# Head pairs of three attentions: the values become the stationary operand, in two column halves of TensorE

## The reference, cut to what matters

```python
# odd layer, selected and window branch (16 heads, groups of 4 share keys and values)
s = einsum(q, k) * scale - slopes * (t - position)
p = masked_softmax(s, causal)
o = einsum(p, v);  o_layer = g0 * o_cmp + g1 * o_slc + g2 * o_win
# second block: memory attention (256 keys) and selected attention (top-k of the causal keys)
p = softmax(einsum(qm, km) * MEM_DH ** -0.5);  out = einsum(p, vm)
p = softmax(where(valid, einsum(qb, kg) * SA_DH ** -0.5, -inf));  out = einsum(p, vg)
```

## Time and profile before

| | |
|---|---|
| median of 3 runs | 1486.98 us (1486.61 to 1489.99) |
| the profiled execution | 1486.23 us, of which its span is 1484.4 us |
| TensorE (PE) busy | 1429.5 us, 96% of the span |
| VectorE, ScalarE, GpSimd busy | 592.7, 600.2, 626.2 us |
| mean granted TensorE clock | 0.991 of full speed |

### The profile page before, as it was taken

The page is one execution under the profiler, slowest core; times in us unless marked ns, Lnnn a source line. Parts: engine busy times, 40 slices in busy tenths (PEclk is TensorE's granted clock), DMA queues, the critical chain, the costliest instruction groups (busy, mean ns, idle before and its releaser), DMA issues.

```text
span 1484.4 us, 20224 instructions
## 1 busy us (share of the span) xinstructions
PE 1429.5 (96%) x7598; PEld 1163.8 (78%) x7601; DVE 592.7 (40%) x1130; ACT 600.2 (40%) x1131; POOL 626.2 (42%) x345
## 2 busy tenths in 40 slices
PE   6999999999999999999999998988999999999999
PEld 4787886878778787888887677877788888888887
DVE  1114104632452255666434678779422322323000
ACT  5112232634123337666434574545334433433210
POOL 3763543654346523233344672621144434444441
PEclk9999999999999999999999999999999999999999
DMA  7543522022234410003033232103023232332330
GB/s 197 118 94 100 124 89 66 1 51 72 85 114 137 119 57 15 21 25 94 29 87 115 85 87 78 57 15 114 15 86 92 93 99 86 95 100 87 99 113 29
DMA packets 78402, 120.28 MB, mean 81 GB/s; under 512 B 8449, under 2 KB 41393, under 8 KB 77937
## 3 DMA queue, kind: packets, MB, share of 16 engines
q1 hardware_dynamic: 76096, 114.21, 26.6%
q0 software_dynamic: 2208, 4.98, 1.2%
q10 hardware_dynamic: 16, 0.00, 0.0%
HBM read 114.95 MB, written 4.19 MB: 80 GB/s over the span
## 4 chain that ended last, share of the span: by engine, by line
PE 79%; issue 7%; POOL 5%; DVE 3%; ACT 2%; DVEq 1%; DMA 1%; POOLq 1%; ACTq 0%; SPq 0%
PE psum L1636 20%; PE psum L1638 19%; PE psum L1637 19%; PE psum L1682 5%; PE psum L1668 3%; POOL weight_low L455 3%; PE psum L1648 3%; PE psum L1615 2%; PE psum L1784 1%; PE psum L1983 1%; PE psum L1959 1%; PE psum L1771 1%; POOL rstd L479 1%; DVEq L1363 1%; DMA x_tokens<-in_x 1%
## 5 line engine op out<-in xcount | busy, mean ns | idle before, releaser
L455 POOL TENSOR_TENSOR weight_low<-weight_raw,weight_high 128x1024 fp32r<-128x1024 f32 x188 | 459.2, 2446 | 613.7 <-ACT weight_high L675 313.8
L1636 PE MATMUL psum<-act_ring,weight_high 128*128 128x512 f32 x704 | 282.4, 401 | 0.4 <-issue 0.4
L1638 PE MATMUL psum<-act_ring,weight_low 128*128 128x512 f32 x704 | 277.3, 394 | 0.0
L1637 PE MATMUL psum<-act_ring,weight_high 128*128 128x512 f32 x704 | 277.0, 394 | 0.0
L675 ACT ACTIVATE weight_high<-weight_raw 128x1024 fp32r<-128x1024 f32 x104 | 109.9, 1060 | 387.3 <-PE psum L1638 378.9
L1636 PE MATMUL psum<-weight_high,act_ring 128*128 128x512 f32 x480 | 193.4, 403 | 2.9 <-DVE odd_k L1243 2.3
L1638 PE MATMUL psum<-weight_high,act_ring 128*128 128x512 f32 x480 | 190.2, 396 | 0.0
L1637 PE MATMUL psum<-weight_low,act_ring 128*128 128x512 f32 x480 | 190.2, 396 | 0.0
L1636 PEld LDWEIGHTS psum<-act_ring,weight_high 128*128 128x128 f32 x704 | 132.4, 188 | 35.7 <-issue 5.1
L1638 PEld LDWEIGHTS psum<-act_ring,weight_low 128*128 128x128 f32 x704 | 132.3, 188 | 34.1
L1637 PEld LDWEIGHTS psum<-act_ring,weight_high 128*128 128x128 f32 x704 | 132.4, 188 | 30.4
(11 more groups left out here) (332 smaller groups left out, 2145.6 us busy)
## 6 DMA issues: line engine op xcount, KB each, us to landing
weight_raw<-in_w_ffn_in SPq DMA_DIRECT2D x88, 256.0 KB
weight_raw<-in_even_w_in SPq DMA_DIRECT2D x32, 512.0 KB
weight_raw<-in_w_in SPq DMA_DIRECT2D x24, 512.0 KB
weight_raw<-in_w_ffn_out SPq DMA_DIRECT2D x22, 512.0 KB
weight_raw<-in_odd_w_in SPq DMA_DIRECT2D x20, 512.0 KB
weight_raw<-in_even_w_out SPq DMA_DIRECT2D x8, 512.0 KB
weight_raw<-in_odd_w_in SPq DMA_DIRECT2D x16, 256.0 KB
weight_raw<-in_odd_w_out SPq DMA_DIRECT2D x8, 512.0 KB
```

The source lines that it names most:

```text
L455: nc.gpsimd.tensor_tensor(WL[:, r], RAW[:, r], WH[:, r].bitcast(f32), ALU.subtract).then_inc(split_ready, 1)
L1636: mm(bank, hi_l, hi_r, start=start, stop=False, skip_group_check=True)
L1637: mm(bank, hi_l, lo_r, start=False, stop=False, skip_group_check=True)
L1638: return mm(bank, lo_l, hi_r, start=False, stop=stop, skip_group_check=True)
```

## The change

In the odd, memory and selected attention (not in the first layer) the two operands of the value products change places. The steps s and s+1 of two neighbouring query tiles make a **half** n of 256 queries. For each block of 128 keys the values (128 x 64) are stationary and the turned probabilities of up to 256 queries stream: h = 0 in columns 0 to 63 of the array, h = 1 in columns 64 to 127. The result is turned: head dimension on partitions (h = 0 on 0 to 63, h = 1 on 64 to 127), 512 queries of a pair along a bank. ScalarE copies that bank to SBUF (`pair_copy`), TensorE turns it back in four transposes (`pair_back`), and VectorE takes the pair as before. In the diff, `pair_copy` is ScalarE's, the lines on `pair_back` with `dve` are VectorE's, and `half_values`, `pair_back` and the loop are TensorE's.

```diff
+        def probs_t(s, h):
+            if s // 2 % 2 == 0:
+                half = A_PT[:, h].rearrange("p a (b q) -> p (a b) q", b=2)
+            elif s < SEC_FIRST:
+                half = O_PT[h]
+            else:
+                half = G_F[:, 4 + 2 * h:6 + 2 * h, :].rearrange("p a (b q) -> p (a b) q", b=2)
+            at = P * (step_tile(s) % 2)
+            return half, half[:, 0:step_width(s) // P, at:at + P]
...
+        def half_free(eng, s):
+            n = (s - FOX_UNITS) // 2
+            if n >= 2:
+                eng.wait_ge(sem("half_values"), n - 1)
+            elif n >= 0:
+                eng.wait_ge(sem("pair_values"), FOX_UNITS)
...
+            def pair_copy(s, first):
+                p, last = divmod(s - 6, 4)
+                if first and s >= first + 6 and last == 0:
+                    act.wait_ge(sem("half_values"), 2 * (p - FOX_UNITS // 4) + 2)
+                    nc.scalar.activation(pair_t(p), PS[:, 6 + p % 2, :], ACT.Copy).then_inc(sem("pair_out"), 1)
...
                 if s >= s0 + 7 and last == 0:
-                    dve.wait_ge(sem("pair_values"), 4 * p + 4)
+                    if s0:
+                        dve.wait_ge(sem("pair_back"), p - FOX_UNITS // 4 + 1)
+                    else:
+                        dve.wait_ge(sem("pair_values"), 4 * p + 4)
...
+            def half_values(n, value):
+                s0 = FOX_UNITS + 2 * n
+                p, late = s0 // 4, n % 2
+                if not late:
+                    pe.wait_ge(sem("pair_done"), p - 1)
+                keys = 2 if SEC_FIRST <= s0 < SEC_FIRST + MEM_UNITS else 2 * late + 2
+                for h in range(2):
+                    pe.wait_ge(sem("pair_pt_b" if h else "pair_pt"), s0 + 2)
+                for t in range(keys):
+                    first = P if t and t == keys - 1 and keys == 2 * late + 2 and s0 not in range(
+                        SEC_FIRST, SEC_FIRST + MEM_UNITS) else 0
+                    for h in range(2):
+                        last = mm(PS[rows_of(h), 6 + p % 2, 2 * P * late + first:2 * P * late + 2 * P], value(h, t),
+                                  probs_t(s0, h)[0][:, t, first:2 * P], start=t == 0, stop=t == keys - 1,
+                                  skip_group_check=True)
+                last.then_inc(sem("half_values"), 1)
+
+            def pair_back(p):
+                pe.wait_ge(sem("pair_out"), p - FOX_UNITS // 4 + 1)
+                for t in range(NT):
+                    last = nc.tensor.transpose(PS[:, 6 + p % 2, P * t:P * t + P], pair_t(p)[:, P * t:P * t + P],
+                                               ID[:, :])
+                last.then_inc(sem("pair_back"), 1)
...
-            for u in range(ODD_UNITS + 3):
+            for u in range(ODD_UNITS + 4):
...
-                if u >= 3:
+                if u >= 4 and u % 2 == 0:
                     i, gp = (u - 3) // 16, (u - 3) // 4 % 4
                     col = 256 * SNAKE[i % 2][gp][0] + HD * i
-                    pair_values(s - 3, lambda h, t, col=col: O_V[:, t, col:col + HD])
+                    half_values(u // 2 - 2, lambda h, t, col=col: O_V[:, t, col:col + HD])
+                if u >= 7 and u % 4 == 3:
+                    pair_back((s - 7) // 4)
```

More of the change, by code:

```diff
@@ L230, in program @@
         lay_b.close()
+        O_PT, O_OT = [None, None], [None, None]
+        lay_b = ExitStack()
+        O_PT[0] = sb(lay_b, "odd_probs_t_a", [P, NT, 2 * P])
+        O_OT[0] = sb(lay_b, "odd_pair_t0", [P, T])
+        lay_b.close()
         W2 = sb(lay_o, "cmp_w2", [P, 2, 2, HD])
@@ L263, in program @@
         G_L = sb(lay_l, "hg_log_forget", [P, 4, T])
+        lay_l.close()
+        lay_l = ExitStack()
+        S_OT = sb(lay_l, "sec_pair_t", [P, 2, T])
         lay_l.close()
@@ L742, in pair_exp @@
                                              sem("pair_probs"), 1)
+                pair_copy(s, first)
             def high(block, i, r):
@@ L918, in _ @@
             act.wait_ge(sem("cmp_taken"), 2 * NT)
-            for s in range(ODD_UNITS + 2):
+            for s in range(ODD_UNITS + 3):
                 pair_exp(FOX_UNITS + s, FOX_UNITS, SEC_FIRST)
@@ L974, in _ @@
                 split_and_take("hg_n", i, G_N[:, :, 512 * i:512 * i + 512], beside_hg, (ACT.Identity, ACT.Silu)[i], "sec")
-            for s in range(SEC_FIRST, SEC_FIRST + MEM_UNITS + SA_UNITS + 2):
+            for s in range(SEC_FIRST, SEC_FIRST + MEM_UNITS + SA_UNITS + 3):
                 pair_exp(s, SEC_FIRST, SEC_FIRST + MEM_UNITS + SA_UNITS)
@@ L1099, in pair_step @@
                     dve.wait_ge(sem("pair_turned"), 2 * k + 1)
-                    if k >= 2:
-                        dve.wait_ge(sem("pair_values"), k - 1)
-                    v.tensor_copy(A_PT[:, k % 2, 0, 0:n], PS[:, 4, 0:n]).then_inc(sem("pair_pt"), 1)
+                    if k >= FOX_UNITS:
+                        half_free(dve, k)
+                        v.tensor_copy(probs_t(k, 0)[1], PS[:, 4, 0:n].rearrange("p (t q) -> p t q", q=P)).then_inc(
+                            sem("pair_pt"), 1)
+                    else:
+                        if k >= 2:
+                            dve.wait_ge(sem("pair_values"), k - 1)
+                        v.tensor_copy(A_PT[:, k % 2, 0, 0:n], PS[:, 4, 0:n]).then_inc(sem("pair_pt"), 1)
                 if s < s0 + steps:
@@ L2085, in _ @@
             pe.wait_ge(sem("sa_features"), 8)
-            for s in range(SEC_FIRST, SEC_FIRST + MEM_UNITS + SA_UNITS + 3):
+            for s in range(SEC_FIRST, SEC_FIRST + MEM_UNITS + SA_UNITS + 4):
                 if s < SEC_FIRST + MEM_UNITS + SA_UNITS:
```

33 lines of the change are left out of this document (24 added, 9 removed).

## The result

The kernel with the change takes a median of 1469.33 us (4 runs, 1468.20 to 1472.47), the kernel before 1488.39 us on the same chip (4 runs, 1486.61 to 1489.99). The ratio is 0.9865, with a 95% interval of 0.9852 to 0.9879: faster by 1.2 to 1.5%. The profiled execution took 1469.13 us; that of before had taken 1486.23, so between the two traces 17.1 us are to be found. (The four runs of before are 1486.6, 1487.0, 1489.8 and 1490.0; two of them lie over 3 us above its profiled one, and so the medians stand 19 apart.)

What follows compares the result with a forecast made beforehand. PE, busy 96% of the span, was taken to bound the kernel; -17 us in the odd layer and -1 in the second block, from 1486.2, gave 1468.5 for the profile and 1469 for the median, range 1462 to 1488.

Steps and rivals of the forecast that it cites:

- What bounds: Whole kernel: PE is busy 96% of the span; the odd layer is PE's alone, the memory attention partly VectorE's.
- Do the column halves run side by side?: New value products: both heads' streams run abreast, as row halves do; early half 0.85 us, late half 1.71.
- Turning back: After each pair's values on PE: four transposes plus the return to the scores' row halves, 0.53 us.
- One change of shape more, 0.1: PE's pair: the step without values goes straight from turning to scores, adding 0.1 us; PE's pair sums to 8.26 us.
- PE waits 0.18 in each pair: Odd layer's 512-key scores: the loop through VectorE and ScalarE takes 5.34 us, PE's work 5.16; the pair takes 8.44.
- waits of PE that rise from 4 to 8 us: Sign of a right forecast in the odd stretch's timeline: PE's waits rise to 8 us or so, most at scores behind exponentials.
- covered by a tenth of a us: ScalarE's new copy: the turning back needs it 0.9 us after the late half, and PE has 1.0 of other work.
- Rival 3: ScalarE's copy tour binds: each pair loses about 0.5 us more, 1477; chance 0.75 together with the forecast.
- Ends and high parts: Odd layer: uncovered stage end +1.7 us, nine steps with high parts +1, first steps without values +0.5; layer -17.
- Second block: Memory attention gains nothing; selected attention gains 2 x 1.4 us, given back by an end of 1.7; sum -1.
- Rival 1: Value products: 64-wide loads stand in the open, +1.3 us a pair; about 1485, no change that can be told; chance 0.09.
- Rival 2: Value products: the column halves run one after another, +0.72 us a pair; 1486.2 + 16 = 1502; chance 0.16.

Runs made afterwards that it cites:

- experiment 1: The change, but both heads write their values to partitions 0 to 63, so both use one column half of the array: 1506.63 us, ratio 1.0119 to the kernel before.
- experiment 8: The change, but TensorE turns every pair back twice, eight transposes in place of four: 1475.99 us, ratio 0.9897 to the kernel before.
- experiment 7: The change without ScalarE's copy and the four transposes back; VectorE takes the turned bank as it is: 1469.42 us, ratio 0.9853 to the kernel before.
- experiment 10: The change without copy and turning back, with VectorE taking a finished odd-layer pair one step later: 1463.28 us, ratio 0.9814 to the kernel before.
- experiment 6: The change, but ScalarE copies each pair's bank twice: 1482.01 us, ratio 0.9946 to the kernel before.
- experiment 5: The change in the odd layer alone; memory and selected attention keep the old way: 1471.69 us, ratio 0.9882 to the kernel before.
- experiment 4: The change, but each query tile streams by itself, 128 columns at a time, 20 passes a pair in place of 12: 1470.18 us, ratio 0.9878 to the kernel before.
- experiment 9: The change, but VectorE takes a finished odd-layer pair one step later, behind the second 256-key maximum: 1469.34 us, ratio 0.9851 to the kernel before.
- experiment 2: The change, but in each half all key blocks of head 0 come first, then all of head 1: 1486.87 us, ratio 0.9986 to the kernel before.

## Why the prediction was right, point by point

The forecast was 1469 for the median and 1468.5 for the profile; they are 1469.33 and 1469.13. (Its own sum, 1486.2 less 18, gives 1468.2.) Faster by over 0.3% had 0.79. The mechanism was right; that the numbers agree within a us is partly luck. The forecast was -18, and the traces are 17.1 apart, the medians 19.1; the median of before has itself risen by 1.4 since the forecast used it, and several terms were off and cancelled. The steps, one by one:

- **What bounds.** That the odd layer is PE's alone held: PE's shorter pair came out whole in the time, 9.70 to 8.44 us.
- **Do the column halves run side by side?** Taken from the row halves, as the nearest row in kind. Right, and better than there: starts 0.01 apart, the streams back to back. The late half was put at 1.71 (1.66), the early one at 0.85 (0.80). The terms of the streams, 1.51 and 0.65, were exact (experiment 1); the 0.2 for the first load and the change of shape is 0.15.
- **Turning back**: 0.53 forecast, 0.58 measured.
- **"One change of shape more, 0.1"** was the mis-sized term. The turning ahead of a half now takes 1.02 for eight transposes and 0.59 for four, where it took 0.93 and 0.49: the first record of a 64-column product starts some 0.1 us later behind a transpose than that of a 128-column one did. No wait for a copy is in this: in experiment 8, where the other engines have more time, they are 1.03 and 0.58. The change has two such places in each pair besides the one counted. TensorE's pair is 8.41 us (experiment 8), not 8.26.
- **"PE waits 0.18 in each pair"** was mis-sized the other way: the wait is 0.03 (8.44 less 8.41). Its sign, waits of PE that rise from 4 to 8 us, most of them at scores behind an exponential, did not come: the rows make 5.5 us where before's make 4.5, and what is new stands in the last pair. The loop itself was priced well: from the 384-key scores to the 512-key scores 5.34 forecast, 5.30 in the timeline (636.04 to 641.34), and experiments 7 and 10 show that it needs 8.43 and that VectorE's taking of the pair, named in the forecast's chain, is in it. The sum 8.44 is right because the pair is the longer of the two, and the loop's was right; the too small value for TensorE stood under it. That is luck: a forecast by TensorE's pair alone would have been 0.15 x 16 = 2.4 us too low. Whether the 0.03 is a wait for the loop or for ScalarE's copy is not told apart.
- **ScalarE's copy "covered by a tenth of a us"**: by 0.02 at most (experiment 6). The forecast let the copy start 0.2 after the late half; it starts 0.38 after, because the second 512-key exponential is in front. Rival 3 was nearer than said.
- **Ends and high parts**: forecast +3.2 against 16 x -1.26. -17 was forecast for the stage, -17.9 measured. The end costs 1.0 us with the last pair's own saving already taken off, where -1.26 + 1.7 = 0.4 was forecast. The first period saved 1.7 (10.66 to 8.99), where 1.26 - 0.5 = 0.8 was forecast; by what the other kernels show of this period, it says little. The steps with high parts cost 0.13 in three pairs and 0.33 in one, of which one pair before had 0.31 as well: +0.4 for the +1 forecast. Experiment 8 shows that they are waits for another engine.
- **Second block**: -1 forecast, -1.0 measured, by other parts. Memory attention was to give nothing and costs 0.5 (the offset goes from -16.05 at its first scores to -15.53 at the selected attention's first), the last 512-key scores stand at -18.16 (-2.6 for the -2.8 forecast), and the end costs 1.1 for 1.7. In the memory attention PE, behind waits of 0.9, 0.3, 0.2 and 1.2 us, ran at a mean clock of 0.66 from 1007 to 1012 us. The values of a half take 1.02 us at the full clock (1003.17 to 1004.19) and 1.91 there (1008.93 to 1010.84):

```profile
1003.17 1.08 PE L1758 MATMUL psum<-pair_probs_t,mem_k_v 128*64 128x256 f32 x8
...
1008.93 1.98 PE L1758 MATMUL psum<-hg_q_f,mem_k_v 128*64 128x256 f32 x8
```

Such a stretch shows in the traces of eleven of the twelve kernels whose second block was changed (not in experiment 1's), and neither in the kernel before nor in experiment 5, which leave that block as it was. So it looks like a cost of the change that no term of the forecast has; no run takes it away alone.
- **What was not foreseen** besides: the stretch at 1.2 GHz between the stages, +1.5 us in this profile. It stands against the 0.9 that the odd stage won beyond its forecast.
- **Rival 1, loads in the open.** Records within a head follow at the pitch of the stream, and experiment 4 adds 16 loads a pair for nothing. The Trainium skill (TensorE: Matmul & The Clock Gate, The mechanism) says that a weight load overlaps a running matmul only where the row groups differ; here all loads share all row groups with two running products, and none shows. The measurement decides against the rule in this form.
- **Rival 2, one after another**: not so, but its price was near (16 us over the kernel before given, 17.8 measured when forced).

## What to carry to other kernels

Where the output of a float32 product has only 64 columns on the stationary side, two independent ones in the two column halves cost the time of one (here with 128 rows, and streams of 128 and 256 columns); put the small operand there, let the long one stream, and alternate between the halves every one to four records; eight in a row cost 0.9 us a half here, and nothing between was tried. Price a change of this kind by the streamed columns at their pitch plus 0.1 us for each new switch between 128- and 64-column products, and the turning back where the layout must be kept.

After TensorE's share is cut, find the length of the next loop before the next cut: adding work to one engine (experiments 6 and 8) and taking it away (7) show in one run each which engine has slack and how much. Here TensorE's 8.41, the loop's 8.43 and ScalarE's copy stood within 0.03 us of each other, so that neither of the two single cuts that were tried (experiments 7 and 9) paid.

## What the runs showed of the hardware

- TensorE starts products out of program order when they use the other column half: in experiment 2 head 1's first record starts at 632.02, ahead of head 0's record at 632.24 and two more. Three waiting records were passed there, and three in the early halves, where head 1 starts beside head 0's first of four; never more in these halves. The Trainium skill (TensorE: Matmul & The Clock Gate, The mechanism) says that matmuls start and end in program order; this trace doesn't agree. A semaphore on the last product of one half would say nothing of the other half's; in the halves looked at here the last product of the program was also the last to start.
- A granted clock that falls in eleven profiles and not in three others, behind the same two waits of PE (0.8 and 1.3 us), moved 1.5 us. Differences of that size between two traces are to be located before they are given to an edit, and looked for in every trace at hand before they are denied to it.
